# Hybrid mixer and top-4-of-32 experts on one core: scatters issued together, final rows requested elsewhere

## The chip, the cores and the metric

One core of a Trainium2 chip runs the whole program. The metric is the device time of one execution in microseconds; of several runs the median counts.

## What is computed

A sequence of 2048 tokens with 1024 columns goes through a mixer (gated linear attention beside a state space scan) and then through a mixture of experts; the last step is an RMS norm of every row. All of it is float32. The part that matters here, cut from the reference:

```python
def moe_ffn(h, router_w, router_b, w_gate, b_gate, w_up, b_up, w_down, b_down):
    top_vals, top_idx = lax.top_k(logits, TOP_K)
    gates = jax.nn.softmax(top_vals, axis=-1)
    ...
    xs = hf[tok]
    gate = lax.ragged_dot(xs, w_gate, group_sizes) + b_gate[sorted_e]
    up = lax.ragged_dot(xs, w_up, group_sizes) + b_up[sorted_e]
    gate = jnp.minimum(gate, SWIGLU_LIMIT)
    up = jnp.clip(up, -SWIGLU_LIMIT, SWIGLU_LIMIT)
    act = (up + 1.0) * (gate * jax.nn.sigmoid(SWIGLU_ALPHA * gate))
    out = lax.ragged_dot(act, w_down, group_sizes) + b_down[sorted_e]
    y = jnp.zeros((t, d), out.dtype).at[tok].add(out * wsel[:, None])
...
        x = x + moe_ffn(h2, ...)
    return rmsnorm(x, final_norm_w)
```

## The kernel before

The first third of the span is the mixer; it leaves the residual rows in DRAM (`xacc_d`, 2048 rows and 128 spare ones), the normed rows (`h2_d`), and a table `tab_d` with, for each expert, the tokens routed to it and their gates. Places of the table that no token fills hold the index of a spare row (2048 and above).

Then the experts run in 32 chunks (the page counts 384 weight units, 12 to a chunk), one expert each, in order of falling size. A chunk has n places, n one of eight `SIZES` from 320 down to 208. Over 256 it is called wide and has three blocks of rows (r = 0, 1, 2), otherwise two (r = 0, 1). Every weight matrix comes in units of 1 MB: q = 0 to 7 are gate and up in turn, q = 8 to 11 are down. For a unit, SP requests it into one of four slots of `raw` (`load`, L510), ACT copies it rounded to `whi` (`hi`, L1274), DVE subtracts to get the rest `wlo` (`lo`, L1864), and PE multiplies with both. SP requests unit q when `lo` of unit q-4 is done. ACT and DVE evict the products from PSUM (`evict`, L1307 and L1887), DVE and ACT form the activations (`activated`, `act_hi`, `act_lo` L1930), and the down products of a narrow chunk are evicted by rows (`evict_rows`, L1902; in the last chunk L1898). PE needs `act_lo` of the last pair of units for the last quarter of its first down unit.

POOL has the indirect DMAs. In chunk i it copies the tables, requests the gather of the next rows (`gather`, L807), and adds the rows of the chunk before to `xacc_d` with one accumulating scatter for each block (`scatter`, L812). Before the scatter of block r it waits until that of block r-1 has landed (`d_sc[r - 1]`, L855): both may hold spare rows. `own_wait` (L680) is a small add on POOL ahead of every such step.

The last chunk (n = 208) is followed by the final norm, and the two overlap. All 2048 rows are normed, in 16 tiles t of 128 rows that lie in buffers that fall free (`rows_at`: xg2, xraw1, xraw0, ybuf2, two parts of yT, halves of the raw slots, work). A tile is requested by SP (`rows_in`, L622, by pairs p of tiles), squared and summed by ACT (`square_rows`, L1325), its root is taken by POOL (`roots`: an add L907 and a power L909, two tiles at a time), it is scaled by DVE (`scaled_rows`, L1954) and sent out by SP (`rows_done`, L627). The rows of the last expert's own tokens are handled apart: POOL gathers them from `xacc_d` (L899) after both scatters have landed, DVE adds the bias part (`own_rows`, L1912) and the products (L1898), ACT squares them (L1366), POOL takes their root last, DVE scales them (L1999), and after all 16 tiles have landed in `out` POOL scatters them over it (L918), which ends the program.

Each engine works through its own list in order. For DVE in the last chunk that list is, for each q: evict(q), activation steps, `lo(q + 4)`; then `own_rows`; then the four `evict_rows` with scaled tiles between them; then the rest of the tiles. SP's list in the last chunk is units 4, 5, 6, 7, 9, 8, the bias row, 10, 11, then the tiles:

```python
            for r in range(2):
                sp.wait_ge(d_sc[r], i * 16 + 32)
            sp.wait_ge(d_sc[2], n_wide * 16 + 32)
            for p in range(3):
                rows_in(p)
```

## Time and profile before

| | |
|---|---|
| median of 3 runs | 3471.32 us (3469.68 to 3473.95) |
| the profiled execution | 3474.84 us |
| its span in the profile | 3473.2 us |
| PE busy | 3411.4 us (98%) |
| DVE, ACT, POOL busy | 62%, 46%, 18% |
| granted TensorE clock, mean | 0.992 |
| transfers | 826.58 MB, 238 GB/s in the mean |

The span is what the profiler saw between the first and the last instruction; the execution's own time is 1.6 us longer. Engines are PE (TensorE), DVE (VectorE), ACT (ScalarE), POOL (GpSimd) and SP (SyncE, which only issues transfers). A row "[idle before <- releaser]" tells how long the engine stood before the instruction, and whose signal came last. Busy spans of POOL are rough. Line numbers are those of the kernel before.

### The profile page before, as it was taken

What the parts mean: (1) busy time and instruction counts of PE and PEld (TensorE: products, weight loads), DVE (VectorE), ACT (ScalarE), POOL (GpSimd) and SP (SyncE); (2) the same over time, 40 slices, a digit from 0 to 9 for tenths busy, and PEclk for the clock granted to TensorE, in tenths of its full rate; (3) what the DMA queues carried; (4) which work ended last, traced back from release to release, by engine and by line L of the source; (5) the groups of instructions that cost most, each with busy time, mean ns of one, the idle gap of its engine ahead of it and who ended that gap; (6) DMA issues with size and microseconds to landing.
All of it is one profiled execution on the core that took longest, in us unless ns stands there. A gap on an engine that the chain in (4) does not pass through costs nothing.

```text
span 3473.2 us, 57451 instructions
## 1 busy us (share of the span) xinstructions
PE 3411.4 (98%) x21623; PEld 3107.6 (89%) x21623; DVE 2139.3 (62%) x2728; ACT 1607.8 (46%) x2047; POOL 637.0 (18%) x848
## 2 busy tenths in 40 slices
PE   7999999999999999999999999999999999999997
PEld 6888888888888999999999999988888888888986
DVE  3565355455456555655566666667777777777777
ACT  4443333333333444444444444455555555555555
POOL 1011111111113111111112111121112112212214
PEclk9999999999999999999999999999999999999998
DMA  9888888887875555555666666567666766776778
GB/s 373 327 311 328 303 286 302 301 291 278 300 275 176 165 174 175 175 175 183 184 197 195 198 185 193 189 211 233 224 209 215 237 226 223 245 230 223 246 240 318
DMA packets 475283, 826.58 MB, mean 238 GB/s; under 512 B 21838, under 2 KB 419294, under 8 KB 458785
## 3 DMA queue, kind: packets, MB, share of 16 engines
q1 hardware_dynamic: 443360, 721.83, 59.4%
q0 software_dynamic: 24320, 75.95, 9.6%
q10 hardware_dynamic: 7488, 27.27, 2.2%
q8 instruction: 73, 1.20, 0.1%
q14 instruction: 42, 0.34, 0.0%
HBM read 726.14 MB, written 98.96 MB: 238 GB/s over the span
## 4 chain that ended last, share of the span: by engine, by line
PE 92%; DMA 2%; DVE 2%; issue 1%; POOL 1%; ACT 1%; SPq 0%; POOLq 0%; DVEq 0%; ACTq 0%
PE pp L2039 14%; PE acc L2460 13%; PE acc L2456 10%; PE acc L2457 10%; PE acc L2458 10%; PE acc L2462 7%; PE pp L2029 5%; PE acc L2472 4%; PE acc L2474 4%; PE acc L2473 3%; PE tpm L2429 2%; PE tp L2008 2%; DMA uraw<-in_w_in 1%; PE tpm L2435 1%; PE seg L2084 1%
## 5 line engine op out<-in xcount | busy, mean ns | idle before, releaser
L1864 DVE TENSOR_TENSOR wlo<-raw,whi 128x2048 fp32r<-128x2048 f32 x384 | 876.0, 2289 | 301.5 <-ACT whi L1274 301.1
L1274 ACT ACTIVATE whi<-raw 128x2048 fp32r<-128x2048 f32 x384 | 730.1, 1910 | 151.7 <-PE acc L2474 103.0
L2460 PE MATMUL acc<-xhl,whi 128*128 128x512 f32 (+3 forms) x2304 | 762.9, 385 | 0.0
L680 POOL TENSOR_TENSOR gate_op<-gate_op 1x1 f32<-1x1 f32 x351 | 170.4, 485 | 2727.3 <-DVE ybuf L1902 532.4
L2462 PE MATMUL acc<-xhl,wlo 128*128 128x256 f32 (+3 forms) x2304 | 625.3, 271 | 0.0
L2456 PE MATMUL acc<-xhl,whi 128*128 128x272 f32 (+3 forms) x1792 | 535.6, 299 | 0.0
L2457 PE MATMUL acc<-xhl,whi 128*128 128x272 f32 (+3 forms) x1792 | 531.0, 296 | 0.0
L2458 PE MATMUL acc<-xhl,wlo 128*128 128x272 f32 (+3 forms) x1792 | 531.0, 296 | 0.0
L2460 PEld LDWEIGHTS acc<-xhl,whi 128*128 128x128 f32 x2304 | 432.3, 188 | 67.0
L1307 ACT ACTIVATE work<-acc,bgu 128x256 f32<-128x256 f32 (+7 forms) x400 | 173.0, 469 | 585.1 <-PE acc L2458 370.6
L2462 PEld LDWEIGHTS acc<-xhl,wlo 128*128 128x128 f32 x2304 | 438.7, 190 | 0.7
L2456 PEld LDWEIGHTS acc<-xhl,whi 128*128 128x128 f32 x1792 | 337.1, 188 | 0.0
L2457 PEld LDWEIGHTS acc<-xhl,whi 128*128 128x128 f32 x1792 | 337.0, 188 | 0.0
L2458 PEld LDWEIGHTS acc<-xhl,wlo 128*128 128x128 f32 x1792 | 336.9, 188 | 0.0
L2039 PE MATMUL pp<-u,hhi 128*128 128x512 f32 x1024 | 326.8, 401 | 4.2 <-DVE zb L1395 4.2
L2456 PE MATMUL acc<-ahl,whi 128*128 128x272 f32 (+3 forms) x896 | 270.0, 301 | 0.0
L2458 PE MATMUL acc<-ahl,wlo 128*128 128x272 f32 (+3 forms) x896 | 265.6, 296 | 0.0
L2457 PE MATMUL acc<-ahl,whi 128*128 128x272 f32 (+3 forms) x896 | 265.5, 296 | 0.0
L2039 PEld LDWEIGHTS pp<-u,hhi 128*128 128x128 f32 x1024 | 190.9, 189 | 45.0 <-DVE zb L1395 4.3
L2472 PE MATMUL acc<-whi,ahl 128*128 128x512 f32 (+3 forms) x576 | 228.8, 397 | 1.2 <-DVE ahl L1930 1.2
L2474 PE MATMUL acc<-whi,ahl 128*128 128x512 f32 (+3 forms) x576 | 225.5, 391 | 0.0
L2473 PE MATMUL acc<-wlo,ahl 128*128 128x512 f32 (+3 forms) x576 | 225.3, 391 | 0.0
(330 smaller groups left out, 5726.2 us busy)
## 6 DMA issues: line engine op xcount, KB each, us to landing
u<-split_d SPq DMA_DIRECT2D x112, 2048.0 KB, 8.8
raw<-in_moe_w_gate SPq DMA_DIRECT2D x128, 1024.0 KB, 4.9
raw<-in_moe_w_up SPq DMA_DIRECT2D x128, 1024.0 KB, 4.9
raw<-in_moe_w_down SPq DMA_DIRECT2D x128, 1024.0 KB, 9.4
split_d<-u SPq DMA_DIRECT2D x16, 2048.0 KB, 13.5
uraw<-in_w_in SPq DMA_DIRECT2D x12, 1024.0 KB, 11.0
yT<-in_moe_b_down SPq DMA_DIRECT2D x18, 512.0 KB
xin<-in_x ACTq DMA_DIRECT2D x14, 512.0 KB, 9.3
```

What stands on the lines that cost most here:

```text
L1274: act.activation(whi[:, q % RING, :, :], raw[:, q % RING, :, :], ACT.Copy).then_inc(a_hi, 1)
L1864: dve.tensor_tensor(wlo[:, q % RING, :, :], raw[:, q % RING, :, :], whi[:, q % RING, :, :].bitcast(F32), ALU.subtract).then_inc(v_lo, 1)
L2029: m = pe.matmul(pp[n % 2][:, c * PW:(c + 1) * PW], w_[:, k, c * P:(c + 1) * P], h_[:, k, :], start=(k == 0 and w_ is wh and h_ is hhi), st ...
L2039: m = pe.matmul(pp[t][:, :], h_[:, 4 * q + k, :], w_[:, k, :], start=(q == 0 and k == 0 and h_ is th and w_ is wh), stop=(q == 1 and k == ...
L2456: pe.matmul(into[:, 0:n], hi_, of[:, k, 0, 0:n], start=(k == 0), stop=False)
L2457: pe.matmul(into[:, 0:n], hi_, of[:, k, 1, 0:n], start=False, stop=False)
L2458: m = pe.matmul(into[:, 0:n], lo_, of[:, k, 0, 0:n], start=False, stop=(k == KD - 1))
L2460: pe.matmul(into[:, 0:2 * n].rearrange("p (c n) -> p c n", c=2), hi_, of[:, k, :, 0:n], start=(k == 0), stop=False)
L2462: m = pe.matmul(into[:, n:2 * n], lo_, of[:, k, 0, 0:n], start=False, stop=(k == KD - 1))
L2472: pe.matmul(into, hi_, whi[:, slots_, k, :], start=(k == 0), stop=False)
L2473: pe.matmul(into, hi_, wlo[:, slots_, k, :], start=False, stop=False)
L2474: m = pe.matmul(into, lo_, whi[:, slots_, k, :], start=False, stop=(k == KD - 1))
```

## The change

- In every chunk, POOL no longer waits for the scatter of block r-1 before it issues that of block r. The scatter gets a bounds check at row 2047, so places with a spare row's index are left out of the transfer.
- In the last chunk SP waits for both scatters right after the bias row, then requests tiles 0 and 1 ahead of unit 10, and tiles 2 and 3 ahead of unit 11.
- In the last chunk `own_rows` runs on DVE after evict(4), ahead of `lo(8)`, and no more after `lo(11)`.
- The roots are taken in six groups (2, 2, 4, 4, 4 tiles and the own rows) in place of nine groups of two; `scaled_rows` waits for the group that holds its tiles.

```diff
--- before.py
+++ after.py
@@ -65,6 +65,7 @@
 UNITS = 12
 RING = 4
 UC = 256
+ROOTS = ((0, 2), (2, 2), (4, 4), (8, 4), (12, 4), (TILES, 2))
 
 
 
@@ -609,6 +610,11 @@
             n_wide, i = chunk_loops(sp, last_chunks(sp), chunk, lambda i: None)
             sp.dma_start(fnw[:, :], final_norm_w.partition_broadcast(P)).then_inc(d_vectors, 16)
             e = expert_of(sp, i)
+
+            def rows_in(p):
+                for t in (2 * p, 2 * p + 1):
+                    sp.dma_start(rows_at[t], xacc_d[t * P:(t + 1) * P, :]).then_inc(d_fin[p], 16)
+
             for q in (4, 5, 6, 7, 9, 8, 10, 11):
                 if q != 8:
                     sp.wait_ge(tiles_known, 1)
@@ -616,23 +622,21 @@
                 load(e, q)
                 if q == 8:
                     bias_row(i, e)
-
-            def rows_in(p):
-                for t in (2 * p, 2 * p + 1):
-                    sp.dma_start(rows_at[t], xacc_d[t * P:(t + 1) * P, :]).then_inc(d_fin[p], 16)
+                    for r in range(2):
+                        sp.wait_ge(v_xl[r], i + 1)
+                    for r in range(2):
+                        sp.wait_ge(d_sc[r], i * 16 + 32)
+                    sp.wait_ge(d_sc[2], n_wide * 16 + 32)
+                    rows_in(0)
+                if q == 10:
+                    rows_in(1)
 
             def rows_done(p):
                 for t in (2 * p, 2 * p + 1):
                     sp.wait_ge(f_dve, t + 3)
                     sp.dma_start(out[0, t * P:(t + 1) * P, :], rows_at[t]).then_inc(d_out, 16)
 
-            for r in range(2):
-                sp.wait_ge(v_xl[r], i + 1)
-            for r in range(2):
-                sp.wait_ge(d_sc[r], i * 16 + 32)
-            sp.wait_ge(d_sc[2], n_wide * 16 + 32)
-            for p in range(3):
-                rows_in(p)
+            rows_in(2)
             for q in range(RING):
                 sp.wait_ge(tiles_known, 1)
                 if q == RING - 1:
@@ -811,7 +815,8 @@
             def scatter(table, r, w):
                 pool.indirect_dma_start(
                     out=xacc_d, out_offset=bass.IndirectOffsetOnAxis(ap=table[0:w, r, 0:1].bitcast(U32), axis=0),
-                    in_=ybuf[0:w, r, :], in_offset=None, compute_op=ALU.add).then_inc(d_sc[r], 16)
+                    in_=ybuf[0:w, r, :], in_offset=None, bounds_check=SEQ - 1, oob_is_err=False,
+                    compute_op=ALU.add).then_inc(d_sc[r], 16)
 
             pool.wait_ge(d_tab0, 16)
             gather(N)
@@ -851,8 +856,6 @@
                 for r, _, _ in rows_of(n):
                     if wide(n):
                         pool.wait_ge(a_y[r], i + 1)
-                    if r:
-                        pool.wait_ge(d_sc[r - 1], i * 16 + 32)
                     own_wait(ran(i, 5 + r, n))
                     scatter(tabb, r, ROWS[r][1])
                 if not wide(n):
@@ -886,11 +889,10 @@
             next_own()
             pool.tensor_copy(tabm[:, :, :], tab[:, :, :]).then_inc(p_tabm, 1)
             for r in range(2):
-                if r:
-                    pool.wait_ge(d_sc[0], i * 16 + 32)
                 next_own()
                 scatter(tabb, r, P)
-            pool.wait_ge(d_sc[1], i * 16 + 32)
+            for r in range(2):
+                pool.wait_ge(d_sc[r], i * 16 + 32)
             pool.wait_ge(p_tabm, i + 1)
             for r in range(2):
                 pool.wait_ge(pe_x[r], i + 1)
@@ -908,9 +910,8 @@
                 pool.wait_ge(f_pool, n_)
                 pool.tensor_tensor(c, b, mhalf[:, 0:count], ALU.pow).then_inc(f_pool, 1)
 
-            for p in range(PAIRS):
-                roots(2 * p, 2, 2 * p + 2, 2 * p + 1)
-            roots(TILES, 2, TILES + 2, 2 * PAIRS + 1)
+            for g, (first, count) in enumerate(ROOTS):
+                roots(first, count, first + count, 2 * g + 1)
             pool.wait_ge(d_out, 32 * PAIRS)
             pool.wait_ge(f_dve, TILES + 4)
             next_own()
@@ -1948,7 +1949,7 @@
             def scaled_rows(p):
                 if p == 0:
                     dve.wait_ge(d_vectors, 32)
-                dve.wait_ge(f_pool, 2 * p + 2)
+                dve.wait_ge(f_pool, 2 * sum(first <= 2 * p for first, _ in ROOTS))
                 for t in (2 * p, 2 * p + 1):
                     k = 2 * TILES + 4 + t
                     dve.scalar_tensor_tensor(out=rows_at[t], in0=rows_at[t], scalar=fst[:, k:k + 1],
@@ -1972,13 +1973,13 @@
                         act_lo(i, n, j)
                     if not final and (q in (7, 8) or q == 9 and wide(n)):
                         x_evict(i + 1, q - 7, n)
+                    if final and q == 4:
+                        own_rows(i, n)
                     if q < 8 or wide(n):
                         lo(i, q + RING)
                     elif not final and q % 2 == 1:
                         lo(i, q + RING - 1)
                         lo(i, q + RING)
-                    if final and q == 7:
-                        own_rows(i, n)
                     if final and q >= 8:
                         for p in ((0,), (1, 2), (3, 4), ())[q - 8]:
                             scaled_rows(p)
@@ -1993,7 +1994,7 @@
             chunk(i, n, True)
             for p in range(5, PAIRS):
                 scaled_rows(p)
-            dve.wait_ge(f_pool, 2 * PAIRS + 2)
+            dve.wait_ge(f_pool, 2 * len(ROOTS))
             for r, _, w in rows_of(n):
                 k = 3 * TILES + 4 + r
                 dve.scalar_tensor_tensor(out=ybuf[0:w, r, :], in0=ybuf[0:w, r, :], scalar=fst[0:w, k:k + 1],
```

POOL at the start of the last chunk, where the rows of the chunk before are added to `xacc_d` and the own rows are gathered into `xg`. Before:

```order
L812 DMA xacc_d<-ybuf,tabb 2176x1024
L890 REGISTER_ALU
L679 REGISTER_ALU [waits d_sc0]
L680 TENSOR_TENSOR gate_op<-gate_op 1x1 [waits gate_ran]
L812 DMA xacc_d<-ybuf,tabb 2176x1024
L679 REGISTER_ALU [waits pe_x0,pe_x1,p_tabm,d_sc1]
L680 TENSOR_TENSOR gate_op<-gate_op 1x1 [waits gate_ran]
L899 DMA xg<-xacc_d,tabm 128x1024
```

and with the change:

```order
L816 DMA xacc_d<-ybuf,tabb 2176x1024
L683 REGISTER_ALU
L684 TENSOR_TENSOR gate_op<-gate_op 1x1 [waits gate_ran]
L816 DMA xacc_d<-ybuf,tabb 2176x1024
L895 REGISTER_ALU
L683 REGISTER_ALU [waits pe_x0,p_tabm,pe_x1,d_sc1,d_sc0]
L684 TENSOR_TENSOR gate_op<-gate_op 1x1 [waits gate_ran]
L901 DMA xg<-xacc_d,tabm 128x1024
```

The wait on `d_sc0` between the two scatters is gone, and the gather's wait now names both. The two gathers' place in the list is the same.

SP in the last chunk, from the bias row on. Before:

```order
L591 DMA yT<-in_moe_b_down 128x1024
L615 REGISTER_ALU [waits tiles_known]
L510 DMA raw<-in_moe_w_down 128x8x256 [waits v_lo]
L615 REGISTER_ALU [waits tiles_known]
L510 DMA raw<-in_moe_w_down 128x8x256 [waits v_lo]
L630 REGISTER_ALU
L632 ISA [waits v_xl1,v_xl0]
L633 ISA [waits d_sc1,d_sc0]
L622 DMA xg<-xacc_d 128x1024 [waits d_sc2]
L622 DMA xraw<-xacc_d 128x1024 x2
L622 DMA ybuf<-xacc_d 128x1024
L622 DMA yT<-xacc_d 128x1024 x2
```

and with the change:

```order
L592 DMA yT<-in_moe_b_down 128x1024
L626 REGISTER_ALU
L628 ISA [waits v_xl1,v_xl0]
L629 ISA [waits d_sc1,d_sc0]
L616 DMA xg<-xacc_d 128x1024 [waits d_sc2]
L616 DMA xraw<-xacc_d 128x1024
L621 REGISTER_ALU [waits tiles_known]
L511 DMA raw<-in_moe_w_down 128x8x256 [waits v_lo]
L616 DMA xraw<-xacc_d 128x1024
L616 DMA ybuf<-xacc_d 128x1024
L621 REGISTER_ALU [waits tiles_known]
L511 DMA raw<-in_moe_w_down 128x8x256 [waits v_lo]
```

The waits for the scatters now stand ahead of the requests for units 10 and 11 (`raw<-in_moe_w_down`), and two tiles go ahead of each of them.

DVE in the last chunk. Before, around the last `wlo` (unit 11) and `own_rows` (`xg<-yT,tabm,xg`):

```order
L1925 SCALAR_TENSOR_TENSOR work<-work 128x2x208 [waits a_sig,v_p]
L1930 TENSOR_TENSOR ahl<-work,ahl 128x2x208 [waits a_ah]
L1863 REGISTER_ALU
L1864 TENSOR_TENSOR wlo<-raw,whi 128x2048 [waits a_hi]
L1908 ISA [waits p_tabm]
L1910 REGISTER_ALU [waits d_bias]
L1912 SCALAR_TENSOR_TENSOR xg<-yT,tabm,xg 128x1024 [waits d_sc0,d_g0]
L1912 SCALAR_TENSOR_TENSOR xg<-yT,tabm,xg 80x1024 [waits d_sc1,d_g1]
L1898 SCALAR_TENSOR_TENSOR ybuf<-acc,tabm,xg 128x512 [waits f_dve,pe_u]
```

and with the change, around evict(4) and the `wlo` of unit 8:

```order
L1887 REGISTER_ALU
L1888 TENSOR_TENSOR work<-work,acc 128x2x208 [waits a_e]
L1909 ISA [waits p_tabm]
L1911 REGISTER_ALU [waits d_bias]
L1913 SCALAR_TENSOR_TENSOR xg<-yT,tabm,xg 128x1024 [waits d_sc0,d_g0]
L1913 SCALAR_TENSOR_TENSOR xg<-yT,tabm,xg 80x1024 [waits d_sc1,d_g1]
L1864 REGISTER_ALU
L1865 TENSOR_TENSOR wlo<-raw,whi 128x2048 [waits a_hi]
L1887 REGISTER_ALU
L1888 TENSOR_TENSOR work<-work,acc 128x2x208 [waits a_e]
```

The two instructions of `own_rows`, with their waits for the gather, moved ahead of the `wlo` of unit 8; nothing else on DVE moved.

## Rows read from the trace of the kernel before

**Rows 1.** The page, engines: busy us, share, instructions.

```profile
PE 3411.4 (98%) x21623; PEld 3107.6 (89%) x21623; DVE 2139.3 (62%) x2728; ACT 1607.8 (46%) x2047; POOL 637.0 (18%) x848
```

**Rows 2.** Waits of PE, 1050 to 3474 us: who waited for whom, us in total, times, longest.

```profile
PE acc L2472 <- DVE ahl L1930: 1.2, 3, 0.8
```

**Rows 3.** Waits of ACT, 1100 to 3474 us.

```profile
ACT whi L1274 <- DMA raw<-in_moe_w_down: 29.8, 11, 4.3
```

**Rows 4.** Waits of POOL, 1100 to 3390 us.

```profile
POOL gate_op L680 <- DMA xacc_d<-ybuf,tabb: 502.2, 74, 9.9
```

**Rows 5.** Timeline of POOL, 3385 to 3474: start, us, operation, [idle before it <- releaser].

```profile
3392.86 2.42 POOL L812 DMA_INDIRECT xacc_d<-ybuf,tabb  x1 [1.34 <-issue]
3402.79 0.45 POOL L680 TENSOR_TENSOR gate_op<-gate_op 1x1 f32<-1x1 f32 x1 [7.51 <-DMA xacc_d<-ybuf,tabb]
3403.44 3.39 POOL L812 DMA_INDIRECT xacc_d<-ybuf,tabb  x1 [0.20 <-issue]
...
3416.37 1.02 POOL L899 DMA_INDIRECT xg<-xacc_d,tabm  x1 [0.54 <-issue]
...
3440.06 3.09 POOL L907 TENSOR_TENSOR fst<-fst,epsx 128x2 f32<-128x2 f32 x1
...
3447.10 1.26 POOL L907 TENSOR_TENSOR fst<-fst,epsx 128x2 f32<-128x2 f32 x1
3448.44 1.62 POOL L909 TENSOR_TENSOR fst<-fst,mhalf 128x2 f32<-128x2 f32 x1
...
3467.05 0.18 POOL L680 TENSOR_TENSOR gate_op<-gate_op 1x1 f32<-1x1 f32 x1 [4.72 <-DMA out<-raw]
```

**Rows 6.** Timeline of DVE, same stretch.

```profile
3418.72 2.29 DVE L1864 TENSOR_TENSOR wlo<-raw,whi 128x2048 fp32r<-128x2048 f32 x1 [3.71 <-ACT whi L1274]
...
3426.36 2.28 DVE L1864 TENSOR_TENSOR wlo<-raw,whi 128x2048 fp32r<-128x2048 f32 x1
3428.76 0.59 DVE L1887 TENSOR_TENSOR work<-work,acc 128x416 f32<-128x416 f32 x1
...
3434.34 2.47 DVE L1912 SCALAR_TENSOR_TENSOR xg<-yT,tabm,xg 128x1024 f32<-128x1024 f32 x2
...
3447.03 2.48 DVE L1954 SCALAR_TENSOR_TENSOR raw<-raw,fst,fnw 128x1024 f32<-128x1024 f32 x2
...
3452.50 0.74 DVE L1898 SCALAR_TENSOR_TENSOR ybuf<-acc,tabm,xg 80x512 f32<-80x512 f32 x1
...
3462.37 2.48 DVE L1999 SCALAR_TENSOR_TENSOR ybuf<-ybuf,fst,fnw 128x1024 f32<-128x1024 f32 x2 [0.59 <-POOL fst L909]
```

**Rows 7.** Timeline of ACT, same stretch.

```profile
3416.77 1.92 ACT L1274 ACTIVATE whi<-raw 128x2048 fp32r<-128x2048 f32 x1 [2.44 <-DMA raw<-in_moe_w_down]
...
3428.61 1.92 ACT L1274 ACTIVATE whi<-raw 128x2048 fp32r<-128x2048 f32 x1
...
3431.50 1.04 ACT L1325 ACTIVATE squares<-xg 128x1024 bf16<-128x1024 f32 x1
```

**Rows 8.** Timeline of SP, same stretch: transfers requested.

```profile
3405.56 1.00 SPq L510 DMA_DIRECT2D raw<-in_moe_w_down  x2
...
3408.89 5.53 SPq L510 DMA_DIRECT2D raw<-in_moe_w_down  x2
3415.64 2.42 SPq L622 DMA_DIRECT2D xg<-xacc_d  x1
```

**Rows 9.** Stretches of 2 us: length, busy us by engine, PEclk, DMA share, GB/s.

```profile
3404.00:3406.00 2.00, 2.00 (x15) 1.99 (x14) 2.00 (x3) 2.00 (x3) 2.00 (x1) 1.00 0.24 78
...
3456.00:3458.00 2.00, 0.00 (x0) 0.00 (x0) 1.77 (x2) 0.00 (x0) 1.92 (x4) 0.50 1.03 420
```

**Rows 10.** The chain that ended last, 3300 to 3474: start, us, what.

```profile
3461.81 5.09 DMA out<-raw
```

**Rows 11.** POOL's operations grouped by line and shape, whole span.

```profile
L701 POOL TENSOR_TENSOR stg<-stg,mhalf 128x4 f32<-128x4 f32 x16 | 18.3, 1142 | 1.3
```

**Rows 12.** The tile xg, 3380 to 3474: from a DMA's issue to its landing.

```profile
DMA to landing us min/median/max: 6.6/7.7/12.0
```


## The prediction

> **What bounds the kernel now.** I read the page first. PE is busy 98% of the span [rows 1], so a change that leaves PE's work alone can gain only where PE waits, or before its first and behind its last product. The waits of PE come second: in the whole expert part it waited 1.2 us for DVE, in three places, and nearly nothing else [rows 2]. POOL stood 502 us in 74 waits for landing scatters, the longest 9.9 us [rows 4], and none of it reached PE. So the scatters' order costs nothing in chunks 1 to 31, and what can move is the last chunk and the norm behind it.
>
> Third, the timelines of the last 90 us. The last product is evicted at 3452.50 [rows 6], 20.7 us before the span ends. ACT squares the 16 tiles from 3431.50 on [rows 7], one in 1.24 us (the square and the read of its sum), through by 3451.4, and the own rows behind the last eviction, by 3454.4. From the first square on POOL and DVE go in turns: the add at 3447.10 ends as DVE's first scaling ends, the power ends 0.55 us after the second scaling [rows 5, 6], and DVE waits 0.59 us for it [rows 6]. A pair of tiles takes 2.48 + 0.59 = 3.07 us. Nine such turns set the end: tile 15 is scaled at 3461.78 and the own rows at 3464.85 [rows 6]. The last tile's transfer lands 5.09 us after its request [rows 10], POOL goes on at 3467.05 [rows 5], and its final scatter ends the span 6.15 us later.
>
> Fourth, the DMA. It is nearly idle in 3404 to 3406 (share 0.24) and full, at 420 GB/s, still in 3456 to 3458 [rows 9]. At that rate a tile (0.52 MB) takes 1.25 us and a unit or two tiles 2.5 us.
>
> **Scatters.** The first one, issued at 3392.86, holds POOL till 3402.79, the second, issued at 3403.44 [rows 5], lands by 3415.64, where SP comes free [rows 8]. With the wait gone, the second is issued at about 3395.8. How long two together take no row shows. From below: 9.9 us after its issue as the first, 3405.7. From above: as late as now, 3415.6, if DVE or the transfers held it back fully. I take 3406.5, near the first, because the second holds at most 80 real rows out of 128 (the chunk before has n = 208) and the DMA has its gap just there [rows 9]. The bounds check I cost at nothing: it adds no instruction, and POOL is idle most of the loop; if it lengthened the 2.4 to 3.4 us of issue, POOL's waits of 502 us cover that in the loop.
>
> In the loop the same work is moved together, so weights can be late. ACT waited 29.8 us for down units, up to 4.3 us at once [rows 3], and PE lost 1.2 us in all [rows 2]. Bounds: -1.2 us if these PE waits went, +1.2 if they doubled. I take 0.
>
> **Gather and own rows.** The gather's first request goes from 3416.37 [rows 5] to about 3407.3, the second to 3408.6. With the middle landing time of 7.7 us [rows 12] both are there by 3416.3, with the shortest (6.6) by 3415.2. DVE reaches `own_rows` when evict(4) ends at 3415.0: before `lo(8)` it stood idle for 3.71 us until 3418.72, since ACT had waited 2.44 us for unit 8 [rows 6, 7]. The two instructions take 2.47 us [rows 6], the second cannot end before the second landing plus 1.24, so `lo(8)` starts at about 3417.5. Cover: that gap. Price if it is gone: `lo(10)` ends at 3428.64, evict(7) starts at 3428.76 [rows 6]; only 0.12 us lie between, and behind evict(7) hang the last activation, PE's last quarter of unit 8 and the squares. So `lo(8)` may start no later than 3418.84, the second landing may be no later than 3417.6, and every us behind that is a us of the end. Taking `own_rows` from 3434.34 frees 2.47 us on DVE there.
>
> **Tiles ahead of units 10 and 11.** SP requested these units within 3408.89 to 3414.4 and the first tile at 3415.64 [rows 8]. Two tiles go ahead of unit 10, two more ahead of 11. Tile 0, requested 1.6 us behind unit 11, took 12.0 us [rows 12], to 3427.6, so unit 11 landed near 3425.5 (an estimate). With the change four tiles more are ahead of it, +5.0 us. What leaves is the second scatter: between 3408 and 3416 it held back the rest by an estimated 3.7 us (2.3 MB were moved where 420 GB/s would move 3.4). Net +1.3, 3426.8; ACT wants it at 3428.61 [rows 7]. Bounds: nothing, if the relief is full, to 5.0 - 3.1 = +1.9 us, if there is no relief. I take 0. Requests go in order of their queue here: tile 0 landed behind the units ahead of it. The Trainium skill says the same of the descriptors in a ring (DMA: Bandwidth & Descriptors, queues, rings and completion order), which speaks against this step; by that rule alone the sum is worse by those 1.9 us.
>
> Squares start at 3431.50 as before: ACT waits there for the activation of unit 7, which PE sets. Tiles are there in time now, so their earlier landing buys nothing itself. It buys a queue that is shorter at the end.
>
> **Roots.** Nine groups become six, 3 x 3.07 us less for POOL. A power over 4 columns took 1.14 us in the mixer [rows 11], so I add 0.4 us for a wide one. Then DVE is late next. Its list from 3437.4: scaled tiles 0 to 3 to 3442.9 with evict(9); tiles 4 to 7 wait for the square of tile 7 at 3441.4, their root ends at about 3443.9; then DVE has four evictions and scalings without a gap: tiles 4 to 7, evict(10), tiles 8 to 11 (root about 3449.5), evict(11), tiles 12 to 15 (root about 3454.5, long before they are due). 12 x 1.24 + 2 x 0.70 us = 16.3, tile 15 at 3460.3, own rows at 3462.8. That is -1.5 us against 3461.78. Evict(11) comes at 3452.1 instead of 3452.50 [rows 6] and no later, so the last squares don't move. Bounds: 0, if POOL gets its turn only where DVE stands (the add at 3440.06 took 3.09 us across three DVE instructions [rows 5]), and -2.2, if the first root comes 1.4 us sooner because `own_rows` no longer stands against it.
>
> **The last transfer.** It took 5.09 us because the queue was still full. With the scatter's 3.7 us gone from the full stretch it should be nearly empty; I take three quarters of the 1.9 us, -1.4, a landing after 3.7 us. Bounds: 0 (still full) and -1.9: the DMA is full to about 3465 (estimated from the landing at 3466.9 less some 1.9 us of fixed time), 3.2 us behind the request, of which the tile's own bytes are 1.25, so 1.9 us are queue. [...] Behind it the 6.15 us to the end stay.
>
> **Sum.** 0 (loop) + 0 (own rows) + 0 (unit 11) - 1.5 (DVE) - 1.4 (last transfer) = -2.9 us. The profiled execution goes from 3474.84 to 3471.9 (span 3470.3). It lies 3.5 us over the median, so for the median 3471.32 - 2.9 = 3468.4 us.
>
> **Rivals.**
> - *Turns stay.* POOL and DVE keep blocking each other, or the queue is still full at the end, so that one of the two terms falls out: -0.5 to -1.5 us, 3470.3. For it: each add and power ends on the end of a DVE instruction [rows 5, 6]. Against it: DVE has work released four tiles at a time. The Trainium skill has a rule for this (SBUF: State Buffer, who interferes with whom): a DVE instruction with two SBUF inputs and a POOL instruction that reads SBUF exclude each other for a whole instruction; the trace agrees with 0.55 us from the end of a scaling to that of a power.
> - *Slower: the gather is late.* The second scatter shares the engines with units 6 and 7 and the first scatter; if it lands after about 3409, the gather lands after 3417.6, DVE stands in `own_rows` ahead of `lo(8)`, and PE waits for the activations. Price: 1 us for 1 us, up to 3426.7 - 3418.8 = 7.9 us at a landing as now. SP stands behind the same scatter ahead of unit 10. With a typical 5 us: 3468.4 + 5 = 3473.4; at most 3476.3. For it: the second scatter landed 12.2 us after its issue [rows 5, 8], which from 3395.8 is 3408.0, a gather at 3417.4.
> - *Unit 11 is late* behind the tiles: +1 to +1.9 us, 3470.
> - *The loop answers*: scatters in 31 chunks crowd weights and PE waits 0.3 us a chunk, +9 us, 3478; or the skipped places take waits away, -1.2 us, 3467.
> - *The change does nothing*: scatters still land one behind the other and the end is set by bytes, 3471.3.
>
> **Chances.** Forecast 48%; turns stay 18%; late gather 14%; unit 11 late 8%; loop 7%; nothing 5%. The range reaches from the forecast with all good bounds (-1.2 - 2.2 - 1.9 = -5.3, 3466, and 1.2 us for the scatter of the runs) to the middle of the late gather: 3464.8 to 3473.2. A measurement of this kernel can tell about 0.2%, 6.9 us, from no change. Faster by more needs all good bounds and more: 5%. Slower by more needs the loop or the late gather at its worst: 5%. Within: 90%.
>
> **What would show it.** In the profile after: POOL's second scatter starts about 3 us behind the first, the gather near 3407; `own_rows` starts at 3415 to 3416.5 and `lo(8)` by 3418.8; ACT's hi(11) near 3428.6 with no wait for DMA; the squares at 3431.5; six roots; DVE without 0.59 us gaps from tile 4 on; the DMA below 400 GB/s after 3455. A start of the squares after 3433, or a wait of PE for DVE above 2 us in the last chunk, would prove the forecast wrong, and a PE total that differs by over 3 us would prove the loop wrong.

## The result and the profile after

| | before | changed |
|---|---|---|
| median of 7 runs | 3472.57 us | 3483.53 us |
| lowest to highest | 3469.68 to 3475.03 | 3478.41 to 3485.77 |
| span of the profiled execution | 3473.2 | 3482.6 |

The ratio is 1.0029, its 95% interval 1.002 to 1.0038: 11 us slower by the medians and 10 by the ratio, where 2.9 us less were forecast and 3473.2 was the end of the range.

The waits of PE in the expert part come first. Changed kernel, 1050 to 3483 us:

```profile
PE acc L2473 <- DVE ahl L1931: 12.8, 14, 1.7
```

Before it was 1.2 us in three places [rows 2], now 12.8 us in fourteen: 11.1 us in thirteen places of the loop, 1.7 us in one of the last chunk. The waits of ACT and of POOL in the same part say where it starts:

```profile
ACT whi L1275 <- DMA raw<-in_moe_w_down: 65.8, 18, 5.7
```

```profile
POOL gate_op L684 <- DMA xacc_d<-ybuf,tabb: 201.1, 29, 9.7
```

ACT waits 65.8 us for down units against 29.8 [rows 3], and POOL 201 us for landing scatters against 502 [rows 4]. POOL got what the change was to give it, and the weights pay for it.

The spans can be cut where a chunk starts, at DVE's copy of the gate and up biases (`bgu`, one in each chunk). The last chunk's copy in the changed kernel:

```profile
3406.58 0.17 DVE L1960 COPY bgu<-mcols 128x16 f32 x1
```

Before it stood at 3395.95. Read so, the two profiles are:

| stretch, us | before | changed |
|---|---|---|
| start to the first chunk (mixer; its code is the same) | 1113.79 | 1111.72 |
| the 31 chunks before the last | 2282.2 | 2294.9 |
| last chunk's start to the end | 77.25 | 76.02 |
| squares start behind that start | 35.55 | 37.15 |

The loop lost 12.7 us and the end won 1.2. In the loop the first 21 chunks, all wide ones among them, last as before (to 0.1 us but for one of +0.9 and the first of -0.8). The last ten, the smallest, last together 659.4 us in place of 646.7: 66.7 to 67.4 for 65.6 in five of six, 65.8 and 66.0 for 63.8, 63.7 and 63.5 for 63.1 and 62.5. That is the whole loss. PE's waits for DVE stand in the same places: in the nine of the ten chunks that got longer, and in no other chunk of the loop.

One of these chunks, the last but one. Before, POOL's scatters, then ACT's first conversion of a down unit, and DVE's of the same unit:

```profile
3343.18 1.80 POOL L812 DMA_INDIRECT xacc_d<-ybuf,tabb  x1 [0.16 <-issue]
...
3354.45 1.57 POOL L812 DMA_INDIRECT xacc_d<-ybuf,tabb  x1 [0.52 <-issue]
```

```profile
3355.43 1.92 ACT L1274 ACTIVATE whi<-raw 128x2048 fp32r<-128x2048 f32 x1 [3.56 <-DMA raw<-in_moe_w_down]
```

```profile
3357.38 2.29 DVE L1864 TENSOR_TENSOR wlo<-raw,whi 128x2048 fp32r<-128x2048 f32 x1 [4.83 <-ACT whi L1274]
```

The same in the changed kernel:

```profile
3352.92 1.80 POOL L816 DMA_INDIRECT xacc_d<-ybuf,tabb  x1 [0.16 <-issue]
...
3356.16 1.58 POOL L816 DMA_INDIRECT xacc_d<-ybuf,tabb  x1 [0.16 <-issue]
```

```profile
3366.08 1.92 ACT L1275 ACTIVATE whi<-raw 128x2048 fp32r<-128x2048 f32 x1 [4.65 <-DMA raw<-in_moe_w_down]
```

```profile
3368.03 2.29 DVE L1865 TENSOR_TENSOR wlo<-raw,whi 128x2048 fp32r<-128x2048 f32 x1 [5.92 <-ACT whi L1275]
```

SP requests units 9 and 8 at 3343.14 before and at 3352.88 now, in both at the moment of the first scatter. The second scatter comes 11.3 us behind the first before, 3.2 us behind it now, while the two units are still on their way. ACT waits 4.65 us for unit 8 in place of 3.56. Against the chunk's start (3333.49 and 3343.05) DVE's part of unit 8 starts at 24.98 in place of 23.89 us, 1.1 us later, and the chunk is 1.1 us longer.

Not every narrow chunk pays for such a delay. Counted from 1, DVE's part of unit 8 starts 1.7 to 2.6 us later than before in chunks 16 to 21 (n = 256), and none of them is longer. In chunks 22 to 27 (n = 240) one is 1.7 us later and not longer; the others are 2.0 to 3.0 us later and 1.1 to 1.9 us longer. Chunks 28 and 29 (n = 224) are 2.4 and 3.3 us later and 2.0 and 2.2 us longer, and chunks 30 and 31 (n = 208) are longer by just what they are later, 0.6 and 1.1 us. So a chunk of 256 places has room for at least 2.6 us, one of 240 for some 1.7, and the smallest have none.

The DMA in the last chunk but one, by stretches of 2 us (the last three numbers are PE's granted clock, the DMA's share and its GB/s), before:

```profile
3347.00:3349.00 2.00, 2.00 (x15) 1.99 (x14) 1.80 (x4) 1.87 (x2) 0.00 (x0) 1.00 0.98 277
3349.00:3351.00 2.00, 2.00 (x15) 1.99 (x15) 2.00 (x2) 0.55 (x1) 0.00 (x0) 1.00 1.10 277
3351.00:3353.00 2.00, 2.00 (x15) 1.99 (x15) 1.55 (x3) 0.76 (x2) 0.00 (x0) 1.00 1.02 236
3353.00:3355.00 2.00, 2.00 (x15) 1.99 (x14) 0.00 (x0) 0.00 (x0) 0.73 (x2) 1.00 1.04 400
```

and in the changed kernel:

```profile
3357.00:3359.00 2.00, 2.00 (x16) 1.99 (x15) 1.90 (x5) 1.49 (x2) 0.81 (x2) 1.00 1.05 278
3359.00:3361.00 2.00, 2.00 (x16) 1.99 (x15) 2.00 (x1) 0.83 (x2) 0.00 (x0) 1.00 1.07 248
3361.00:3363.00 2.00, 2.00 (x15) 1.99 (x14) 1.11 (x3) 0.43 (x2) 0.00 (x0) 1.00 1.06 234
3363.00:3365.00 2.00, 2.00 (x16) 1.99 (x15) 0.00 (x0) 0.00 (x0) 0.00 (x0) 1.00 1.05 295
3365.00:3367.00 2.00, 2.00 (x16) 1.99 (x15) 0.00 (x0) 0.92 (x1) 0.00 (x0) 1.00 1.04 389
```

The DMA is full in both, but while scatters are served beside weights it moves 234 to 295 GB/s and otherwise some 390 to 400. That slow part is 6 us long before and 8 us now, and it ends 19.5 us behind the chunk's start before and 22 us now. Unit 8 pays for that.

The end. DVE in the last chunk:

```profile
3428.83 2.48 DVE L1913 SCALAR_TENSOR_TENSOR xg<-yT,tabm,xg 128x1024 f32<-128x1024 f32 x2 [3.19 <-DMA yT<-in_moe_b_down]
3431.23 2.28 DVE L1865 TENSOR_TENSOR wlo<-raw,whi 128x2048 fp32r<-128x2048 f32 x1
...
3468.40 2.48 DVE L1955 SCALAR_TENSOR_TENSOR work<-work,fst,fnw 128x1024 f32<-128x1024 f32 x2 [1.17 <-POOL fst L911]
```

`own_rows` started 3.19 us after DVE was free, and what it waited for was not the gather but the bias row, requested at 3417.49 and landed 11.2 us later. The two gathers, requested at 3417.18 and 3418.50, took 8.6 and 8.5 us, so they had landed by 3427.0. `lo(8)` follows at 24.65 us behind the chunk's start, where it was at 22.77 [rows 6], and the squares are 1.6 us late. Then the roots, and the last transfer in the chain:

```profile
3455.22 1.01 POOL L911 TENSOR_TENSOR fst<-fst,mhalf 128x4 f32<-128x4 f32 x1
...
3464.19 3.09 POOL L909 TENSOR_TENSOR fst<-fst,epsx 128x4 f32<-128x4 f32 x1
...
3476.22 0.18 POOL L684 TENSOR_TENSOR gate_op<-gate_op 1x1 f32<-1x1 f32 x1 [4.78 <-DMA out<-raw]
```

```profile
3473.30 2.77 DMA out<-raw
```

A power over four columns takes 1.01 us, but the add of the last wide group stood for 3.09 us while DVE ran, and DVE then waited 1.17 us for it (the row of 3468.40). The last tile lands 2.77 us after its request, against 5.09 [rows 10]. The DMA shows why; in the changed kernel it has room at the end, where before it was full at 420 GB/s [rows 9]:

```profile
3468.00:3470.00 2.00, 0.00 (x0) 0.00 (x0) 1.60 (x2) 0.00 (x0) 1.92 (x4) 0.50 0.69 283
```

### The profile page after: what moved, and what is told of

Read it like the earlier page. It is cut to its first block, busy times and chain, and to the rows that moved or that the text cites. A ratio compares the mean times of both kernels' runs of the same rounds, so it can differ in the third digit from the quotient of the medians.

```text
span 3482.6 us, 57473 instructions
## 1 busy us (share of the span) xinstructions
PE 3407.2 (98%) x21623; PEld 3101.2 (89%) x21623; DVE 2136.7 (61%) x2728; ACT 1607.3 (46%) x2047; POOL 625.7 (18%) x839
## 3 DMA queue, kind: packets, MB, share of 16 engines
q0 software_dynamic: 24320, 71.29, 8.4%
## 4 chain that ended last, share of the span: by engine, by line
PE 55%; DVE 5%; DMA 4%; issue 3%; ACT 2%; DVEq 0%; POOL 0%; SPq 0%; POOLq 0%; ACTq 0%
PE acc L2457 10%; PE acc L2458 10%; PE acc L2459 10%; PE acc L2461 7%; DMA raw<-in_moe_w_down 4%; PE acc L2463 3%; PE acc L2473 3%; PE acc L2474 3%; PE acc L2475 3%; DVE wlo L1865 2%; ACT whi L1275 2%; PE tpm L2430 2%; PE tpm L2436 1%; DVE work L1888 1%; DVE work L1922 1%
## 5 line engine op out<-in xcount | busy, mean ns | idle before, releaser
L684 POOL TENSOR_TENSOR gate_op<-gate_op 1x1 f32<-1x1 f32 x348 | 182.6, 525 | 2755.0 <-DVE ybuf L1903 655.3
L2473 PE MATMUL acc<-whi,ahl 128*128 128x512 f32 (+3 forms) x576 | 229.5, 398 | 12.9 <-DVE ahl L1931 12.8
```

Source lines behind the costliest of these rows:

```text
L684: pool.tensor_tensor(gate_op[0:1, 0:1], gate_op[0:1, 1:2], gate_op[0:1, 1:2], ALU.add).then_inc(gate_ran, 1)
L2473: pe.matmul(into, hi_, whi[:, slots_, k, :], start=(k == 0), stop=False)
```

## The experiments

Theory 1: in the narrow chunks the second scatter now runs beside the down units 9 and 8, makes unit 8 late, and ACT, DVE and PE hang on that. Theory 2: the bounds check makes scatters or POOL slower. Theory 3: the wide chunks or the new last chunk make the loss. The start of the first chunk wandered from 1108.0 to 1113.8 us between the profiles, with the same mixer, and the first chunk itself took 83.3 to 87.1 us; both are more than the end can win. So three stretches are compared beside the medians: the 31 chunks, the last ten of them (the small ones), and the end. With the same last chunk as before the end took 77.25, 77.57 and 77.85 us, so a difference under 0.6 us there counts only where a row explains it. A single run has no ratio; it is read by its stretches alone. Line numbers differ by a few between kernels.

| kernel | ratio to before (interval) | loop, us | its last ten chunks | end, us | PE waits for DVE, us |
|---|---|---|---|---|---|
| before | 1 | 2282.2 | 646.7 | 77.25 | 1.2 |
| changed | 1.0029 (1.002 to 1.0038) | 2294.9 | 659.4 | 76.02 | 12.8 |
| a_skip_only | 0.9999 (0.9989 to 1.0008) | 2281.7 | 646.3 | 77.57 | 1.0 |
| b_narrow_serial | 1.0003 (0.9993 to 1.0013) | 2279.3 | 645.7 | 75.77 | 1.9 |
| c_loop_only | 1.0037 (1.0024 to 1.0049) | 2295.2 | 659.9 | 77.85 | 12.5 |
| d_scatters_first | 0.9991 (0.9982 to 1.0001) | 2282.1 | 645.3 | 75.35 | 1.2 |
| k_second_left_out | single run | 2283.8 | 645.9 | 79.10 | 1.9 |
| n_first_serial | single run | 2280.6 | 645.3 | 74.68 | 0.2 |
| f_first_bias | 0.9993 (0.9984 to 1.0002) | 2280.7 | 645.3 | 75.45 | 1.3 |
| h_own_rows_back | single run | 2282.5 | 645.3 | 75.14 | 0.6 |
| g_roots_only | single run | 2282.6 | 645.3 | 74.81 | 0.2 |
| j_roots_nine | single run | 2280.9 | 645.3 | 75.46 | 0.2 |
| l_best | 0.9989 (0.998 to 0.9998) | 2281.6 | 645.4 | 74.67 | 0.2 |
| m_roots_seven | 0.9988 (0.9979 to 0.9997) | 2280.2 | 645.3 | 74.88 | 0.2 |

**Only the bounds check (a_skip_only).** The kernel before with

```diff
-                    in_=ybuf[0:w, r, :], in_offset=None, compute_op=ALU.add).then_inc(d_sc[r], 16)
+                    in_=ybuf[0:w, r, :], in_offset=None, bounds_check=SEQ - 1, oob_is_err=False,
+                    compute_op=ALU.add).then_inc(d_sc[r], 16)
```

> The kernel before with only the bounds check on the accumulating scatters; each still waits for the one before it. Theory 1 (the loss in the narrow chunks comes from the second scatter running beside the requests for units 9 and 8): no loss here, 3471 to 3474 us, PE's waits for DVE in the expert part 0 to 1.5 us as before. Theory 2 (the bounds check makes the scatters or POOL slower, or the skipped places change the traffic for the worse): PE's waits rise to some 12 us and the time to about 3480.

Measured 3469.58 us against 3470.47. POOL's queue moved 71.29 MB in place of 75.95, so the empty places were left out, and the time is the same. Theory 2 falls.

**Narrow chunks one behind the other again (b_narrow_serial).** The changed kernel with

```diff
                 for r, _, _ in rows_of(n):
                     if wide(n):
                         pool.wait_ge(a_y[r], i + 1)
+                    if r and not wide(n):
+                        pool.wait_ge(d_sc[r - 1], i * 16 + 32)
```

> The changed kernel, but in the narrow chunks of the loop the second scatter again waits for the first; wide chunks and the last chunk stay changed. Theory 1: the intervals of the narrow chunks return to 62.5 to 69 us, PE's waits to about 1.2 us, the time falls by 10 to 12 us to about 3471.5. Theory 2 (bounds check): stays near 3483. Theory 3 (the wide chunks' scatters or the new last chunk make the loss): stays within 2 us of 3483.

Measured 3470.19 us: the loop is at 2279.3 us, and the last narrow chunks are at 65.6, 64.2, 63.8, 62.1 and 62.1 again. What remains of PE's waits:

```profile
PE acc L2475 <- DVE ahl L1933: 1.9, 2, 1.6
```

The longest of the two waits, 1.6 us, is in the last chunk, where the squares start 36.96 us behind its start in place of 35.55. One wait, in the narrow chunks, undoes the loss. The wide chunks' scatters are together in this kernel and cost nothing, so theory 3 falls for them, and the new last chunk gains 1.5 us in this profile.

**The loop alone (c_loop_only).** The kernel before with the bounds check and without the wait for `d_sc[r - 1]`; the last chunk as before.

> The kernel before with the scatters beside each other in the loop (and the bounds check); the last chunk as before. Theory 1: the whole loss without what the last chunk gained, about +12 us, 3484 to 3485. Theory 3 (last chunk): 3472.

Measured 3483.32 us, +13 us. The loop lost 13.0 us and the end, unchanged, stayed at 77.85:

```profile
PE acc L2471 <- DVE ahl L1929: 12.5, 13, 1.7
```

**Scatters first (d_scatters_first).** In the narrow chunks both scatters, beside each other, go ahead of the table copy, the table load and the gather:

```diff
                 pool.wait_ge(p_tabb, i + 1)
+                k = 2
+                if not wide(n):
+                    for r in range(2):
+                        own_wait(ran(i, 2 + r, n))
+                        scatter(tabb, r, ROWS[r][1])
+                    k = 4
-                own_wait(ran(i, 2, n))
+                own_wait(ran(i, k, n))
                 pool.tensor_copy(tabm[:, :, :], tab[:, :, :]).then_inc(p_tabm, 1)
...
-                for r, _, _ in rows_of(n):
-                    if wide(n):
+                if wide(n):
+                    for r, _, _ in rows_of(n):
```

> The changed kernel, but in the narrow chunks of the loop both scatters are issued beside each other right after the rows are ready, ahead of the table load and the gather, some 12 us earlier than now, where the DMA is idle. Theory 1 (what hurts is the place beside units 9 and 8, not that the two run together): PE's waits fall to 1 us or below and the time to 3470 to 3472. Rival (two accumulating scatters together are what hurts, wherever they stand): PE still waits over 8 us, 3480 or more.

Measured 3468.19 us. The two accumulate together as in the changed kernel, and the loop shows no loss. Their place, and the weights, in the last chunk but one:

```profile
3323.99 3.46 POOL L816 DMA_INDIRECT xacc_d<-ybuf,tabb  x1 [0.63 <-issue]
...
3328.35 1.58 POOL L816 DMA_INDIRECT xacc_d<-ybuf,tabb  x1 [0.16 <-issue]
```

```profile
3347.95 1.92 ACT L1281 ACTIVATE whi<-raw 128x2048 fp32r<-128x2048 f32 x1 [1.50 <-DMA raw<-in_moe_w_down]
```

The wait for unit 8 is 1.50 us where it was 3.56 before and 4.65 in the changed kernel; all waits for down units fell to 12.2 us. The scatters are served ahead of the requests for units 9 and 8, but not in an idle stretch of the DMA, as I had expected: SP has requested unit 7 (`raw<-in_moe_w_up`) by then. Its requests, and stretches of 2 us (columns as above):

```profile
3328.17 0.37 SPq L511 DMA_DIRECT2D raw<-in_moe_w_up  x1
3337.68 1.00 SPq L511 DMA_DIRECT2D raw<-in_moe_w_down  x2
```

```profile
3324.00:3326.00 2.00, 2.00 (x16) 1.99 (x14) 2.00 (x2) 1.42 (x1) 2.00 (x1) 1.00 0.00 0
...
3330.00:3332.00 2.00, 2.00 (x16) 1.99 (x14) 1.14 (x1) 1.98 (x5) 1.16 (x4) 1.00 1.04 213
3332.00:3334.00 2.00, 2.00 (x16) 1.99 (x15) 1.97 (x3) 1.85 (x2) 0.08 (x1) 1.00 1.04 217
3334.00:3336.00 2.00, 2.00 (x15) 1.99 (x14) 1.93 (x4) 0.55 (x1) 0.00 (x0) 1.00 1.02 255
```

The idle stretch is over when the scatters' bytes move, and the rate is as low beside units 6 and 7 as it was beside 9 and 8. Unit 7 lands 11.3 us after its request, where it was 6.2 before. But ACT converts it only at 3341.53, 2 us behind its landing, and waits for nothing there. The place does no harm because the units beside it have room, not because the DMA is free.

**The second scatter left out (k_second_left_out).** The changed kernel; in the narrow chunks of the loop the second block's rows are not added (8 bytes go to a spare row in their place).

```diff
-                    scatter(tabb, r, ROWS[r][1])
+                    if wide(n) or r == 0:
+                        scatter(tabb, r, ROWS[r][1])
+                    else:
+                        pool.dma_start(xacc_d[SEQ + 8:SEQ + 9, 0:2], spare[0:1, :].bitcast(F32)).then_inc(d_sc[r], 16)
```

> The changed kernel, where in the narrow chunks of the loop the second scatter is left out (an 8 byte write to a spare row stands in its place, so those rows' sums are missing). If the bytes of the second scatter beside units 9 and 8 make the loss: PE's waits for DVE fall from 12.8 us to 1.2 us or less, and the time to about 3471. If the loss is POOL's order or issue (something that any second transfer there causes), they stay above 8 us.

The narrow chunks are back at 65.6, 63.8, 62.7 and 62.1 us, so the second scatter's transfer makes the loss, and not just any second request at that place. Whether its bytes, the number of its rows or the adding count is not told apart. PE's waits are 1.9 us, of which 1.4 are in the last chunk. The one time was 3475.51 and not 3471. POOL's last wait ended at 69.24 us of the end stretch, 9.9 us ahead of the end of the span, in place of 6.4 in the changed kernel, and the first chunk took 87.1 us. This is a single run, and the cause of both stays open.

**Scatters first, one behind the other (n_first_serial).** As l_best below, with

```diff
                     for r in range(2):
+                        if r:
+                            pool.wait_ge(d_sc[0], i * 16 + 32)
                         own_wait(ran(i, 2 + r, n))
```

> As l_best, but in the narrow chunks of the loop the second scatter waits for the first again; both still stand ahead of the table load and the gather. If running them together buys nothing in the loop and only their place counts: narrow chunks of 65.6, 63.8 and 62.1 us, the loop 2280 to 2283 us as in l_best, PE's waits below 1.2 us. If one behind the other pushes the gather or the second scatter into units 9 and 8 again: narrow chunks longer by 0.5 us or more each.

The last ten chunks take 645.3 us as in d_scatters_first, and PE's waits are 0.2 us. In the loop nothing is won by running the scatters together; only where they stand matters.

**The bias row earlier (f_first_bias).** As d_scatters_first, with

```diff
-                if q == 8:
+                if q == 7:
                     bias_row(i, e)
+                if q == 8:
                     for r in range(2):
```

> The kernel with the scatters first in narrow chunks, and in the last chunk the bias row is requested right after unit 7, ahead of units 9 and 8. Theory (own_rows ahead of unit 8's rest waited for the bias row, 3.2 us in the changed kernel, and that moved the squares from 35.55 to about 37 us behind the chunk's start): own_rows starts within 1 us of evict(4), the squares return to 35.5 us, the stretch from the last chunk's start to the end falls from 75.4 to about 74 us, and the time by 1.4 us to about 3467. Rival (it then waits for the gather or unit 8 instead): the squares stay at 36.5 or later and the stretch at 75 us.

The rival won. The bias row was there, and `own_rows` waited for the gather, twice:

```profile
3414.57 1.28 DVE L1920 SCALAR_TENSOR_TENSOR xg<-yT,tabm,xg 128x1024 f32<-128x1024 f32 x1 [1.55 <-DMA xg<-xacc_d,tabm]
3416.86 1.28 DVE L1920 SCALAR_TENSOR_TENSOR xg<-yT,tabm,xg 80x1024 f32<-80x1024 f32 x1 [1.00 <-DMA xg<-xacc_d,tabm]
3418.06 2.28 DVE L1872 TENSOR_TENSOR wlo<-raw,whi 128x2048 fp32r<-128x2048 f32 x1
```

ACT waited 3.13 us for unit 8 besides, `lo(8)` began 24.1 us behind the chunk's start, and the squares at 36.61. The end stretch is 75.45 us, no better than 75.35.

**own_rows where it was (h_own_rows_back).** As d_scatters_first, with `own_rows` behind `lo(11)`:

```diff
-                    if final and q == 4:
-                        own_rows(i, n)
                     if q < 8 or wide(n):
                         lo(i, q + RING)
...
+                    if final and q == 7:
+                        own_rows(i, n)
```

> As the kernel with the scatters first, but own_rows is back behind unit 11's rest; roots and the tiles ahead of units 10 and 11 stay changed. The squares start at 35.55 us behind the chunk's start as before, if only own_rows moved them; at 36.5 or later, if the tiles ahead of unit 11 did. The end by my working: 75.0 us, as the 1.2 us from the squares come back and DVE pays 2.5 us for own_rows where it mostly waits for roots.

The squares start 35.95 us behind the chunk's start, against 36.56 in d_scatters_first and 35.55 before. So some 0.6 us of the delay came from the moved `own_rows`, and 0.4 us from the tiles ahead of unit 11, for which ACT now has to wait:

```profile
3427.95 1.92 ACT L1281 ACTIVATE whi<-raw 128x2048 fp32r<-128x2048 f32 x1 [0.91 <-DMA raw<-in_moe_w_down]
```

**Only the roots (g_roots_only).** As h_own_rows_back, and the tiles are requested behind unit 11 as before.

```diff
-                    rows_in(0)
-                if q == 10:
-                    rows_in(1)
...
-            rows_in(2)
+            for p in range(3):
+                rows_in(p)
```

(The three waits ahead of `rows_in` went back with it.)

> The kernel with the scatters first in narrow chunks; in the last chunk only the roots in six groups are kept: own_rows is back behind unit 11's rest and the tiles are requested behind unit 11 as before. The stretch from the last chunk's start to the end was 77.25 us before and 75.4 to 76.0 with all three edits. If the roots make the gain: 75.5 to 76.5. If the tiles ahead of the weights make it (a queue that is empty sooner): 77 or more.

The end takes 74.81 us, less than either case expected, with the squares at 35.55. The last tile's transfer starts 65.50 us behind the chunk's start (3395.39), where it was 65.86 before, and takes as long as in the changed kernel:

```profile
3460.89 2.77 DMA out<-raw
```

Neither the tiles ahead nor the moved `own_rows` was worth anything: the end went 75.35, 75.14, 74.81 as they were taken out, and the squares 36.56, 35.95, 35.55.

**Nine groups (j_roots_nine).** As g_roots_only with

```diff
-ROOTS = ((0, 2), (2, 2), (4, 4), (8, 4), (12, 4), (TILES, 2))
+ROOTS = tuple((2 * p, 2) for p in range(8)) + ((TILES, 2),)
```

> As l_best, but with the nine groups of before: in the last chunk nothing is changed but the scatters beside each other. If the second scatter out of the full stretch of the DMA shortens the last transfer by itself: it lands 3 to 3.7 us after its request in place of 5.09 and the stretch is 75.3 to 75.9 us. If the roots do it: about 5 us and 77 us.

75.46 us. All that differs from before in this last chunk are the two scatters beside each other, with their bounds check (which alone gained nothing, 77.57 us): 1.8 us of the 2.4 come from them (77.25 to 75.46), 0.65 from the roots (to 74.81; 0.8 to l_best's 74.67). The last tile's transfer lands 2.7 us after its request, with nine groups too, so the shorter queue comes from the scatters and not from the roots. The final wait of POOL is no longer for that transfer, but for the scaling of the own rows:

```profile
3459.05 0.18 POOL L682 TENSOR_TENSOR gate_op<-gate_op 1x1 f32<-1x1 f32 x1 [2.73 <-DVE ybuf L2004]
```

**Seven groups (m_roots_seven).** As g_roots_only with `(12, 2), (14, 2)` in place of `(12, 4)`.

> As l_best, but the last four tiles' roots are taken in two groups of two. In all profiles with a last group of four its add took 3.1 us (it stood while DVE ran three instructions) and DVE then waited 1.17 us. If an earlier group of two gets its turn sooner: the gap of 1.17 us goes, the stretch falls from 74.8 to 73.6 us. If POOL gets its turn only when DVE stands: the gap stays, 74.8 to 75.4 us.

The gap moved and stayed, 74.88 us. POOL and DVE:

```profile
3446.84 4.96 POOL L682 TENSOR_TENSOR gate_op<-gate_op 1x1 f32<-1x1 f32 x1
3451.76 0.18 POOL L913 TENSOR_TENSOR fst<-fst,epsx 128x2 f32<-128x2 f32 x1
```

```profile
3446.90 2.47 DVE L1959 SCALAR_TENSOR_TENSOR raw<-raw,fst,fnw 128x1024 f32<-128x1024 f32 x2
3449.28 2.47 DVE L1959 SCALAR_TENSOR_TENSOR work<-work,fst,fnw 128x1024 f32<-128x1024 f32 x2
3452.76 2.48 DVE L1959 SCALAR_TENSOR_TENSOR raw<-raw,fst,fnw 128x1024 f32<-128x1024 f32 x2 [1.00 <-POOL fst L915]
```

A POOL add over one element took 4.96 us while DVE ran four scalings in a row, and ended when they did.

**The version that is left (l_best).** The kernel of g_roots_only, timed.

> The kernel that keeps only two things: scatters beside each other, issued first in the narrow chunks, and the roots in six groups. In one profile its stretch from the last chunk's start to the end was 74.8 us against 77.25 before, and no narrow chunk was longer. Expected 2.4 us less than before, ratio 0.9993. If the loop's earlier scatters cost something that one profile didn't show: ratio 1.000 or above.

3467.74 us against 3471.71, ratio 0.9989 (0.998 to 0.9998): 4 us faster than the kernel before. In the profiles the end stretch gives 2.6 us of it and the last ten chunks 1.3 (645.4 for 646.7): with the scatters first they are shorter than before, which was not expected. m_roots_seven measured the same (0.9988).

## Why the prediction was wrong

- *"The scatters' order costs nothing in chunks 1 to 31"* is the step that failed, and with it the bounds of -1.2 and +1.2 us for the loop. I took PE's small waits (1.2 us) beside ACT's large ones (29.8 us) for room. They were the edge. In the last chunk I had worked out that `lo(8)` may be late by 0.12 us and no more; the other small chunks have the same order on DVE, and there I didn't ask. The runs showed in its place: the second scatter makes DVE's part of unit 8 late, by 0.6 to 3.3 us in the ten smallest chunks, and these are longer by 1.3 us in the mean (12.8 / 10), the loop by 12.7. c_loop_only and b_narrow_serial show it alone and undone. Of the signs named, the PE total (12.8 us for 1.2) says the loop is wrong, and the squares, 37.15 us behind the chunk's start, lie just past the limit set for them (3433 is 37.05).
- *The loop rival* had the right place and nearly the right price (+9 us, 3478), but 7%. Its price was spread over 31 chunks; it fell on the last ten, of which nine paid. What I should have looked at is who requests what at 3343.14 and 3343.18: the down units and the first scatter in the same 0.1 us, while the old wait kept the second scatter out of the units' way.
- *Bounds check at nothing*: right (a_skip_only, 0.9999), though it took 4.7 MB out.
- *Scatters of the last chunk*: taken as landed at 3406.5, 10.5 us behind the chunk's start. They landed 9.6 us after the issue of the second, 9.9 us behind the start in the changed kernel and 9.4 to 10.1 in the other kernels that have the two beside each other. Right.
- *Own rows*: wrong. I priced the gather and left out the bias row, whose wait stands in the rows of the order ahead of the two instructions (`d_bias`). It took 11.2 us. With it early the gather, which was requested later there, was late instead (f_first_bias). So in both kernels one of the two transfers missed the gap on DVE. The gather's own price was low too, 8.5 and 8.6 us where I took 7.7.
- *Unit 11*: taken as 0, bound +1.9. h_own_rows_back shows 0.4 us on the squares. The relief of 3.7 us in this sum does not follow from the two amounts beside it: 3.4 less 2.3 MB at 420 GB/s are 2.6 us, and the net is then +2.4 in place of +1.3 (3427.9, still ahead of the 3428.61 at which ACT wants the unit). The Trainium skill's rule on a ring's order (DMA: Bandwidth & Descriptors, queues, rings and completion order) points the right way here; ACT waited 0.91 us for unit 11.
- *Roots*: -1.5 forecast, -0.65 and -0.8 measured (j_roots_nine against g_roots_only and l_best). The bound had the reason, POOL gets its turn late when DVE has work in a row: 3.09 or 3.10 us for the last wide add in every kernel with six groups. In the term as I had it, the time at which the last tile is scaled, g_roots_only gains only 0.4 us (65.50 us behind the chunk's start for 65.86), and the changed kernel loses 0.9 (66.72), as its squares are 1.6 us late.
- *Last transfer*: -1.4 forecast, -2.3 measured in the changed kernel (5.09 to 2.77), past my bound of -1.9. That bound took 1.9 us of fixed time, which no run shows; of the 2.77 us the tile's bytes take 1.25 at 420 GB/s, so at most 1.5 us are left for it.
- The end stretch should have been -2.9 us; it was -1.2 in the changed kernel (+0.9 - 2.3, and +0.2 for the final scatter), and -2.4 without the two edits that cost (g_roots_only: -0.4 - 2.3 + 0.2). So the end was forecast 1.7 us too well and the loop 12.7 us too well; the miss is the loop's.

## What to carry to other kernels

A wait that costs its own engine hundreds of microseconds may still hold back traffic that would delay someone else: before taking it away, list what every other queue requests in the time that it kept free, and look how late the first user of those loads may be. Small waits on the bounding engine are no sign of room; room is the gap between the end of the work before and the start of the work that must not be late, and it has to be read in each kind of stage, here also in the small chunks: a delay of 2.6 us cost nothing with 256 places, one of 0.6 us cost 0.6 us with 208. Work that is moved into an engine's idle time takes all its waits along, and each must be met there.

## What the runs showed of the hardware

- Accumulating scatters of at most 128 rows of 4 KB beside weight units of 1 MB: the DMA's share stays at 1.0 and its rate falls to 234 to 295 GB/s beside the down units and to 213 to 255 beside units 6 and 7 (d_scatters_first), from 390 to 400 without them. What that costs depends on who waits for the unit: nothing beside unit 7, up to 2.2 us a chunk beside unit 8.
- Places left out by the bounds check save bytes (4.66 MB, with the same 24320 packets) but no time in this kernel (a_skip_only, ratio 0.9999).
- A one-element add on POOL took 4.96 us (m_roots_seven; POOL's spans are rough) while DVE ran two-input operations back to back, and the add of the last wide group 3.09 or 3.10 us in all nine kernels with six groups. The Trainium skill (SBUF: State Buffer, who interferes with whom) lets the loser wait for a whole instruction; the trace agrees in kind, but here it was four in a row. That the shared port held the add is argued from these times; no run tests it.
- The same mixer code took between 1108.0 and 1113.8 us in the 14 profiles, which alone spreads a whole run by 0.17%.
